# A product that nothing reads, ahead of each group of small products in the second inversion of an RWKV-7 layer

## The reference, cut to what matters

```
def step(S, inp):
    r_t, w_t, k_t, v_t, a_t, b_t = inp
    sa = jnp.einsum('bhvk,bhk->bhv', S, a_t)
    S = S * w_t[:, :, None, :] + sa[..., None] * b_t[:, :, None, :] + v_t[..., None] * k_t[:, :, None, :]
    return S, jnp.einsum('bhvk,bhk->bhv', S, r_t)
```

## Time and profile before

| | |
|---|---|
| median of 3 runs | 1481.44 us (1475.76 to 1487.31) |
| the profiled execution | 1473.81 us |
| its span, first to last instruction | 1472.0 us |
| mean granted TensorE clock in it | 0.933 of full speed |
| TensorE busy with products | 1283.7 us, 87% of the span |
| VectorE busy | 898.5 us, 61% |
| ScalarE busy | 481.0 us, 33% |
| GpSimd busy | 306.2 us, 21% |

### The profile page before, as it was taken

One profiled execution on the slowest core, in us unless ns is written; L12 is line 12 of the kernel. 1 busy time (PEld: TensorE's weight loads), 2 busy tenths in 40 slices (PEclk: granted clock), 3 DMA queues, 4 the chain that ended last, 5 costly groups with the idle time before them and its releaser, 6 DMA issues. The chain is left out here.

```text
span 1472.0 us, 20569 instructions
## 1 busy us (share of the span) xinstructions
PE 1283.7 (87%) x8466; PEld 1067.4 (73%) x8466; DVE 898.5 (61%) x1194; ACT 481.0 (33%) x823; POOL 306.2 (21%) x156
## 2 busy tenths in 40 slices
PE   5999999979868988987997999999933598999698
PEld 4677888868658966866886888887722577888587
DVE  5267763851056667237978456686988788265831
ACT  5234244231327662213242212225462312222400
POOL 2223221221013355013131112122400400000420
PEclk9999999989979999999999999999975799789899
DMA  6212211320120030431242241611200000010523
GB/s 190 44 43 54 47 33 43 115 85 31 64 101 2 1 130 29 146 97 44 87 115 88 79 110 30 193 58 37 79 15 1 1 1 2 2 58 1 201 85 114
DMA packets 117558, 97.79 MB, mean 66 GB/s; under 512 B 37016, under 2 KB 102680, under 8 KB 117336
## 3 DMA queue, kind: packets, MB, share of 16 engines
q1 hardware_dynamic: 103832, 77.45, 17.8%
q10 hardware_dynamic: 13632, 19.01, 4.0%
HBM read 70.23 MB, written 24.51 MB: 64 GB/s over the span
## 5 line engine op out<-in xcount | busy, mean ns | idle before, releaser
L172 PE MATMUL banks<-xt_lo,w_hi 128*128 128x512 f32 x816 | 323.6, 397 | 6.3 <-POOL w_lo L521 6.3
L173 PE MATMUL banks<-xt_hi,w_lo 128*128 128x512 f32 x816 | 320.0, 392 | 0.0
L174 PE MATMUL banks<-xt_hi,w_hi 128*128 128x512 f32 x816 | 319.7, 392 | 0.0
L521 POOL TENSOR_TENSOR w_lo<-features,w_hi 128x1024 fp32r<-128x1024 f32 x55 | 149.6, 2721 | 525.5 <-ACT w_hi L531 525.5
L172 PEld LDWEIGHTS banks<-xt_lo,w_hi 128*128 128x128 f32 x816 | 154.6, 189 | 42.0 <-POOL w_lo L521 6.4
L174 PEld LDWEIGHTS banks<-xt_hi,w_hi 128*128 128x128 f32 x816 | 154.6, 189 | 33.0
L173 PEld LDWEIGHTS banks<-xt_hi,w_lo 128*128 128x128 f32 x816 | 154.7, 190 | 31.3
L580 ACT ACTIVATE temporaries<-banks 128x1024 f32<-128x1024 f32 x47 | 56.0, 1192 | 328.1 <-PE banks L174 319.3
L172 PE MATMUL banks<-xt_lo,eout_mh 128*128 128x512 f32 x128 | 52.0, 407 | 11.4 <-DVE xt_lo L1693 5.7
L172 PE MATMUL banks<-xt_lo,oout_mh 128*128 128x512 f32 x128 | 51.1, 399 | 11.9 <-DVE xt_lo L1693 11.9
L300 PE MATMUL banks<-temporaries,features 128*128 128x128 f32 x256 | 36.8, 306 | 27.4 <-DVE temporaries L277 27.4
(11 more groups left out here) (501 smaller groups left out, 2599.4 us busy)
## 6 DMA issues: line engine op xcount, KB each, us to landing
features<-in_even_w_in SPq DMA_DIRECT2D x26, 512.0 KB, 4.1
features<-in_odd_w_in SPq DMA_DIRECT2D x25, 512.0 KB, 4.6
features<-in_x SPq DMA_DIRECT2D x8, 512.0 KB, 7.7
even_gates<-temporaries ACTq DMA_DIRECT2D x8, 512.0 KB, 2.6
features<-even_gates SPq DMA_DIRECT2D x8, 512.0 KB, 8.7
features<-in_even_w_out SPq DMA_DIRECT2D x8, 512.0 KB, 3.7
temporaries<-in_x SPq DMA_DIRECT2D x8, 512.0 KB, 4.9
h_between_layers<-features SPq DMA_DIRECT2D x8, 512.0 KB, 3.2
```

The costliest lines, as they stand in the source:

```text
L172: nc.tensor.matmul(out, w[0], x[1], start=start, stop=False)
L173: nc.tensor.matmul(out, w[1], x[0], start=False, stop=False)
L174: return nc.tensor.matmul(out, w[0], x[0], start=False, stop=stop)
L521: nc.gpsimd.tensor_tensor(wl[n % 2], wr[n % NW], wh[n % 2].bitcast(F32), ALU.subtract).then_inc(low, 1)
```

## The change

`invert` gets a parameter `unused`, off by default, and a helper `unread(bank)` of the same form as the one in `r7_state`. With `unused=True`, one such product stands ahead of each of the 12 groups (two `y`, two `z`, four `yy`, four `zz`), behind the waits of its group, and writes the bank that the group writes to. Only the inversion of half 1 is called with it.

```diff
-def invert(co, tag, store, at, first_bank=0, four=False, pace=lambda t: t, paces={}, ready=None, free=None):
+def invert(co, tag, store, at, first_bank=0, four=False, pace=lambda t: t, paces={}, ready=None, free=None, unused=False):
...
+        def unread(bank):
+            if unused:
+                nc.tensor.matmul(co.ps[:, bank, :].rearrange("p (a b) -> p a b", b=32), co.hot_r[:, 0:1].to_broadcast([P, P]),
+                                 co.hot_r.rearrange("p (o b) -> p o b", o=1).to_broadcast([P, 16, 32]), start=True, stop=True)
+
         def yy(g):
             pe.wait_ge(x10_out, 2)
             pe.wait_ge(z_out, 4)
             if g >= 2 and not four:
                 pe.wait_ge(zz_out, g - 1)
+            unread(of_group(g))
...
         def zz(g):
             pe.wait_ge(yy_out, g + 1)
+            unread(of_group(g))
...
             pe.wait_ge(x_ready, 1)
             if h and not four:
                 pe.wait_ge(y_out, 2)
+            unread(pair[h][0])
...
             if h and not four:
                 pe.wait_ge(z_out, 2)
                 pe.wait_ge(x10_out, 1)
+            unread(pair[h][0])
...
-    side_by_side(co, clearing(co, at=4), r7_state(co, first), invert(co, "ri1", second.n_st, R7_INVERT[1], pace=lambda t: 1.5 * t))
+    side_by_side(co, clearing(co, at=4), r7_state(co, first), invert(co, "ri1", second.n_st, R7_INVERT[1], pace=lambda t: 1.5 * t, unused=True))
```

## The result

The change made the kernel slower: 1482.94 us in the median of 20 runs (1473.47 to 1496.59), against 1474.22 us in 20 runs of the kernel before (1469.42 to 1487.31). The ratio is 1.0054, with a 95% interval of 1.0032 to 1.0076, so some 8 us. The ratio compares fast runs alone, without the slowest of the changed kernel (1496.59 us), and isn't the ratio of the two medians, which lie 8.7 us apart. The profiled execution took 1479.96 us, with a span of 1478.2 us.

What follows compares the result with a forecast made beforehand. The prediction took TensorE, busy 87% of the span and partly at its lower clock, as the bound. Added products +3.3 us, clock -3.1 us, block 3 -0.5 us gave -0.3 us on 1480.5 us: 1480.2 us, range 1470 to 1490 us.

Steps and rivals of the forecast that it cites:

- What the clock gives back: Half 1's inversion: clock rises near 1258 us, some 10 us sooner, giving 3.1 us; start of block 3 gives 0.5 us.
- Rival 3: Clock rises sooner, falls again at the first yy group's wait, low to the stage's end: +5.0 us, 1485.5 us; chance 0.12.
- rival 4: Later work moves by a microsecond or two, later falls land otherwise: some 6 us either way, on top of each case.
- The price of a product: Twelve products in half 1's inversion: 0.26 us each at full clock, 0.42 us at the lower; sum 3.3 us.
- the upper bound of 4.7 us: Most the added products could cost: three at 0.59 us and nine at 0.32 us.
- The lower clock: Low stretch in half 1's inversion: 0.31 us lost per microsecond at 1.2 GHz, 7.5 us over 23.90 us.
- The fall near 1244 us: At the second y group's 2.25 us wait for ScalarE: the clock still falls there despite the change.
- Block 3: Its start, low for 10.2 us of 14.60 us, worth 3.2 us: 0.5 us taken as given back.
- Rival 1: Added products change nothing for the clock in half 1's inversion; only their price stays: +3.3 us, 1483.8 us; chance 0.22.
- Rival 2: Clock rises right after the second y group, block 3's start gains half: -6.2 us, 1474.3 us; chance 0.16.

Runs made afterwards that it cites:

- e2: The change with only the four products ahead of y and z, those of yy and zz taken out: 1476.55 us, 0.9984 of the kernel before.
- e9: The change plus five unread products ahead of the wait of the first yy group: 1474.42 us, 0.9970 of the kernel before.
- e10: The kernel before plus five unread products ahead of the wait of the first yy group, none of the twelve: 1472.57 us, ratio 0.9970.
- e12: The kernel before, unchanged, profiled a second time: 1483.57 us in one run.
- e8: The change plus eight unread products ahead of the second y group's wait and five ahead of the first yy group's: 1469.83 us, 0.9949 of the kernel before.
- e4: The kernel before plus eight unread products ahead of the second y group's wait and five ahead of the first yy group's: 1465.92 us, ratio 0.9942.
- e6: The change with 32 columns instead of 512 in each of the twelve products: 1482.25 us, 1.0015 of the kernel before.
- e5: The change with only the eight yy and zz products, each 128 columns on the 64x64 array quarter its group leaves alone: 1469.64 us, 0.9963 of the kernel before.
- e7: The kernel before plus eight unread products ahead of the second y group's wait only: 1466.67 us, ratio 0.9937.
- e11: The kernel before plus eight unread products ahead of the second y group's wait, five each ahead of the first yy and second z groups' waits: 1467.09 us, 0.9925.
- e1: The change with only the eight products ahead of yy and zz, those of y and z taken out: 1484.88 us, 1.0035 of the kernel before.
- e3: The change with all twelve products ahead of their groups' waits, in a free PSUM bank: 1482.58 us, 1.0042 of the kernel before.

## Why the prediction was wrong

The forecast was -0.3 us; the kernel became some 8 us slower. Its measured time lies in the range, since that had room for other falls of the clock, but the sign of the sum was wrong. That 1482.94 us lies only 2.7 us from the 1480.2 us forecast is luck: the start of 1480.5 us was taken from four executions (their median is 1478.6 us; 1481.44 us is that of three), and 20 runs put the median of before at 1474.22 us, 6.3 us lower. As a change it was +8.7 us between the medians against -0.3 us.

**The step that failed is "What the clock gives back", with its -3.1 us.** The first profile of before was read as if it were the kernel: a fall, one rise, then full clock to the end of the block. The rise was moved to an earlier time, near 1258 us, and what lies behind it was left as it was. In the changed kernel's profile neither held. The low stretch ended at 1270.0 us, after 27.3 us; the block of tokens with both z groups took 22.24 us (1244.69 to 1266.93 us), where 18.5 us were forecast; and a second low stretch of 13.7 us followed. In place of 3.1 us given back, block 2 had 17.1 us more at the lower clock than in the first profile of before, and just as much as in the second. The rise after 6.8 us, sooner than the forecast had it, stands in e2 and e9, two of the three profiles with 512-column products behind the waits of y and z and the second y group's wait not filled (the change is the third), and in none of the seven others with that wait not filled. So the added products may bring it, but not dependably.

And a clock that has risen must be held, and ahead of the first yy group it often wasn't. Filling that one wait is worth 8.5 us in the changed kernel (e9) and 1.7 us to 4.5 us in the one before (1472.57 us in e10, against 1474.22 us in the first set and 1477.06 us in its own). What is left between e9 and e10 is 1.9 us. So of the 8.7 us between the medians some 7 us are the second fall, which the change seems to meet more often (17 of its 20 runs are above 1478 us, against 7 of 20 of before), and 2 us the twelve products, less what they give back in other places. This split takes medians of different sets together, each uncertain by some 4 us; that the larger part hangs on that wait is shown by e9 against the change, the exact share isn't.

**Rival 3 was this mechanism, and got 0.12.** Its place was right: a second fall between 1269 and 1276 us (1273.4 us measured), low until near the end of the stage (13.7 us against the 15.4 us taken). Its time of 1485.5 us is 2.6 us off, by the same luck of the start: +5.0 us was its change. And it had the clock rise sooner first, which the changed kernel's profile doesn't show. What spoke against it was that in the one trace the clock held at that wait. The three times shown of before, 1475.76 to 1487.31 us, with the profiled execution at 1473.81 us, were put down to falls elsewhere in rival 4; by e10 and e12 a good part came from this place: e12 is 9.8 us longer than the first profiled execution, 7.9 us of it in block 2.

**The price of a product was mis-sized.** Taken were 0.26 and 0.42 us and a sum of 3.3 us; 4.15 us (the change against e12) and 4.8 us (e8 against e4) were measured, about the upper bound of 4.7 us. The rows taken for the bounds, 0.32 and 0.59 us, were too low themselves: 0.41 to 0.43 us and 0.70 us went by from an added product to its group. The distance between two unread products in a row was the wrong row to read: the second of them needs no small product's weight load behind it. Ahead of the tail groups it was 0.50 us, of which e6 shows 0.28 us to be the break alone. The Trainium skill (TensorE: Matmul & The Clock Gate, "Part 3: Packing small matmuls — row/col tiling") says that a weight load overlaps a running product only if the two use different groups of rows of the array. The traces agree: 0.41 to 0.43 us to the group's first product behind one on all rows, 0.01 to 0.06 us in e5 behind one on the other rows.

**The lower clock costs more than taken.** 0.31 us for each of its microseconds rests on the estimate that a z group takes 1.80 us at full clock, by its number of records. In e4 it takes 1.21 us, so it loses 0.72 us and not 0.13 us, and the prediction's own sum becomes (6.45 + 1.44) / 21.30 = 0.37 us. e4 gives 0.36 us, and e12 0.46 us, where the second low stretch lies over the yy and zz groups. Those take 16 records in 1.97 us instead of 1.14 us.

**The fall near 1244 us stays, as forecast,** and for the reason given, since the product stands behind the wait. The first y group's product was indeed hidden: the wait went from 2.25 us to 2.08 us.

**Block 3** was right in sign and small in the sum: 0.5 us taken of 3.2 us. In the changed kernel's profile the clock held over its first 13.60 us, so the whole 3.2 us were there; in e8 3.4 us at the lower clock stood there against e4's 10.2 us. But e12, the kernel before, was low there for 17.1 us (1294.80 to 1311.90 us above), so this place differs between executions of one kernel too, and that the twelve products bring the gain isn't shown. (The 5 tenths that the prediction read near 1290 us are the slice from 1104 to 1141 us, in the inversion of half 0; no sum uses them, and no run here touched that place.)

**Rival 1** (no effect on the clock, +3.3 us) isn't refuted: the change and e12 have the same three stretches and differ by 4.15 us. Its 1483.8 us is the nearest number of all, by the same luck of the start. Only the 6.8 us of e2 and e9 speak against it. **Rival 2** (the clock hardly stays down) came true in e4, e7 and e11, by other means than the change's.

**What stays open** is why the changed kernel meets the second fall more often. With only 32 columns (e6), only yy and zz (e1), only y and z (e2) or ahead of the waits (e3) it showed in the profile as well; in e5, whose products leave the timing of block 2 alone, and in e7 it didn't. In the nine profiles in which the wait ahead of the first yy group isn't filled and a rise comes before it, one thing goes with the fall: the time from the rise of the clock to the start of that wait (in e3 the 0.80 us that the added product leaves of it).

| run | rise | wait from | between | what followed |
|---|---|---|---|---|
| before, e5, e7 | 1268.2, 1268.6, 1261.0 | 1271.07, 1271.42, 1263.37 | 2.9, 2.8, 2.4 us | held to the end of block 2 |
| e1 | 1262.0 | 1264.91 | 2.9 us | fell 6.8 us after the rise |
| the change, e12, e2, e6 | 1270.0, 1270.9, 1271.0, 1272.5 | 1271.73, 1272.24, 1272.41, 1273.75 | 1.7, 1.3, 1.4, 1.2 us | fell 3.4 us after the rise |
| e3 | 1271.1 | 1273.02 | 1.9 us | fell 3.4 us after the rise |

So with 1.2 to 1.9 us between them the clock fell in all five profiles, with 2.4 to 2.9 us in one of four. How long the first low stretch lasts, 23.9 us or 27.3 us, sets this in part, and the kernel before has both. That the added products shift the odds by delaying the groups is likely, but was only argued; several profiles of each kernel would test it.

## What to carry to other kernels

In this kernel a product that nothing reads helped TensorE's clock most where TensorE waits; over the whole array and between groups of work it cost more than it gave. So put such products ahead of the wait, as many as fit into it, in a bank that is free. Read which wait comes just before the fall, and fill that one. Eight products in one place gave 0.6%, twelve spread over the work cost 0.5%. Before the clock of a stage is taken from one profile, compare its time with the spread of the runs: if that is 10 us or more, the stage may have two courses, and the profile shows one.

## What the runs showed of the hardware that was not expected

- TensorE's clock stayed at 1.2 GHz through 27.30 us in which a product was running in every microsecond. Busy time alone doesn't bring it back. The Trainium skill (TensorE: Matmul & The Clock Gate, "What's actually happening") speaks of how busy TensorE has recently been; here that some product always ran wasn't enough.
- A wait of 2.25 us was enough to lose the clock for over 20 us, and the same wait with 0.43 us of product in it (e3) as well; filled to 0.17 us (e4, e7) it wasn't lost there.
- A product over the other quarter of the array, ahead of each yy and zz group (e5), cost nothing that block 2 shows, and the kernel was 0.4% faster than before (0.9963, 0.9935 to 0.9992), with all 12 runs under 1473 us: the second fall seems not to have occurred in any. Why is open: in its one profile the clock runs as in the first profile of before.
